# Weight tiles of the second half of the value product, split into buffers of their own

## What is computed

```python
x = x + 0.5 * swiglu(rms_norm(x, p['ffn1_norm']), p['ffn1_w_in'], p['ffn1_w_out'])
h = rms_norm(x, p['mix_norm'])
q, k, v, f, bx_in, by_in, sb, sc, sx, g = split_columns(h @ p['w_in'])
logf = jax.nn.log_sigmoid((f + p['b_forget']).astype(jnp.float32))
o_a = attn_fn(q, k, v, logf)          # logits get c[t] - c[s], c = cumsum(logf)
```

## Time and profile before

| | |
|---|---|
| median of three runs | 3013.25 us (3011.82 to 3015.27) |
| the profiled execution | 3012.57 us |
| its span in the profile | 3010.9 us |
| mean granted TensorE clock | 0.991 |
| busy: PE, DVE, ACT, POOL | 98%, 49%, 33%, 4% |
| HBM over the span | 82 GB/s |

### The profile page before, as it was taken

The page is one execution under the profiler, slowest core; times in us unless marked ns, Lnnn a source line. Parts: engine busy times, 40 slices in busy tenths (PEclk is TensorE's granted clock), DMA queues, the critical chain, the costliest instruction groups (busy, mean ns, idle before and its releaser), DMA issues.

```text
span 3010.9 us, 54957 instructions
## 1 busy us (share of the span) xinstructions
PE 2959.2 (98%) x21632; PEld 2862.5 (95%) x21632; DVE 1465.2 (49%) x2025; ACT 985.3 (33%) x1287; POOL 119.0 (4%) x104
## 2 busy tenths in 40 slices
PE   7999998999999999999999999989999999999999
PEld 6999998888899999999999999988888999999998
DVE  4434355555744544343444444566665454444434
ACT  4212133444633342121332111334445333321113
POOL 1000011000000010000100000100000000000001
PEclk9999999999999999999999999999999999999999
DMA  3222222333222222222222222223332222222222
GB/s 116 84 85 79 77 82 81 84 82 82 71 82 79 91 84 83 75 80 84 85 84 73 88 86 78 84 69 83 81 82 80 84 84 91 73 86 80 84 84 87
DMA packets 299022, 248.82 MB, mean 83 GB/s; under 512 B 20643, under 2 KB 296307, under 8 KB 298919
## 3 DMA queue, kind: packets, MB, share of 16 engines
q1 hardware_dynamic: 296775, 242.44, 26.0%
q0 software_dynamic: 2144, 4.98, 0.5%
HBM read 240.04 MB, written 7.34 MB: 82 GB/s over the span
## 4 chain that ended last, share of the span: by engine, by line
PE 94%; DVE 2%; ACT 1%; issue 1%; DVEq 0%; DMA 0%; POOLq 0%; ACTq 0%; SPq 0%
PE ps L448 85%; PE ps L671 2%; PE ps L616 2%; PE ps L700 1%; DVE tmp L1019 1%; PE ps L661 1%; PE ps L647 1%; PE ps L594 1%; PE ps L617 1%; PE ps L603 0%; PE ps L552 0%; PE ps L553 0%; PE ps L554 0%; DMA xin<-in_x_sample 0%; ACT whi L759 0%
## 5 line engine op out<-in xcount | busy, mean ns | idle before, releaser
L759 ACT ACTIVATE whi<-wraw 128x1024 fp32r<-128x1024 f32 (+1 forms) x456 | 475.1, 1044 | 1610.1 <-PE ps L448 1560.9
L448 PE MATMUL ps<-hh,whi 128*128 128x288 f32 x4480 | 967.1, 298 | 18.5 <-ACT vtok L857 6.1
L448 PE MATMUL ps<-hh,wlo 128*128 128x288 f32 x4480 | 961.9, 296 | 0.0
L448 PE MATMUL ps<-hl,whi 128*128 128x288 f32 x4480 | 961.5, 296 | 0.0
L1013 DVE TENSOR_TENSOR wlo<-wraw,whi 128x1024 fp32r<-128x1024 f32 (+1 forms) x456 | 548.4, 1205 | 457.4 <-ACT whi L759 456.3
L448 PEld LDWEIGHTS ps<-hh,whi 128*128 128x128 f32 x4480 | 724.9, 190 | 25.1 <-ACT vtok L857 6.3
L448 PEld LDWEIGHTS ps<-hh,wlo 128*128 128x128 f32 x4480 | 724.5, 189 | 0.0
L448 PEld LDWEIGHTS ps<-hl,whi 128*128 128x128 f32 x4480 | 724.3, 189 | 0.0
L1047 DVE TENSOR_TENSOR tmp<-tmp,ps 128x576 f32<-128x576 f32 x176 | 132.7, 754 | 509.3 <-PE ps L448 508.4
L448 PE MATMUL ps<-al,whi 128*128 128x288 f32 x1408 | 302.2, 296 | 0.0
L448 PE MATMUL ps<-ah,whi 128*128 128x288 f32 x1408 | 302.1, 296 | 0.0
(11 more groups left out here) (282 smaller groups left out, 2519.8 us busy)
## 6 DMA issues: line engine op xcount, KB each, us to landing
wraw<-in_ffn_w_in SPq DMA_DIRECT2D x88, 1024.0 KB
wraw<-in_ffn_w_out SPq DMA_DIRECT2D x32, 1024.0 KB
wraw<-in_w_in SPq DMA_DIRECT2D x28, 1024.0 KB
wraw<-in_w_in SPq DMA_DIRECT2D x56, 512.0 KB
wraw<-in_ffn_w_out SPq DMA_DIRECT2D x16, 768.0 KB
wraw<-in_w_branch SPq DMA_DIRECT2D x24, 512.0 KB
wraw<-in_w_out SPq DMA_DIRECT2D x9, 1024.0 KB
kv<-in_cache_k SPq DMA_DIRECT2D x128, 64.0 KB, 1.9
```

The source lines that it names most:

```text
L448: last = pe.matmul(ps[slot][:, half, 0:HF], weights, rhs[:, k, half * HF:(half + 1) * HF], start=(start and c == 0 and n == 0), stop=(stop ...
L759: act.activation(split_tile(whi, j, rowwise), raw_tile(slot, j, rowwise), ACT.Copy).then_inc(hi_ready, 1)
```

## The change

Two buffers `vhi` and `vlo` are added, of the shape of `whi` and `wlo`. They are laid over the last part of `kpt` and over `prob`; a placeholder `over_kv` keeps them off `kv` and off `kpt`'s first 512 columns. `values(1)` reads them in place of `whi` and `wlo`. Value tiles 2 and 3 are split into them right behind ffn1, ahead of the square root on ScalarE (with no wait for PSUM) and ahead of its reciprocal on VectorE. The first pair's tiles 0 and 1 take the places at which value tiles 2 and 3 were split, after `values(0)`. Nothing is added to or taken from the computation, the transfers or the number of splits. SyncE's program is the same; what it waits for (`lo_ready`) comes at other times.

```diff
             with ExitStack() as m2:
+
+                sb("over_kv", [P, SB * NPG * P + SEQ], F32, m2)
+                vhi = sb("vhi", [P, 2, KD * P], F32R, m2)
+                vlo = sb("vlo", [P, 2, KD * P], F32R, m2)
+            with ExitStack() as m2:
                 oh = sb("oh", [P, 12, N], F32R, m2)
...
-                            rh = whi[:, :, k * P:(k + 1) * P]
-                            rl = wlo[:, :, k * P:(k + 1) * P]
+                            rh = (whi, vhi)[u][:, :, k * P:(k + 1) * P]
+                            rl = (wlo, vlo)[u][:, :, k * P:(k + 1) * P]
...
-            def split_ahead(st, w, k, L, i=0):
-
-                wait_tile(st, k, L, i)
+            def split_ahead(st, w, k, L, i=0, into=whi):
+
+                if k is not None:
+                    wait_tile(st, k, L, i)
...
                 ffn("ffn1", 0, L)
+                fv = S["fv"]
+                split_ahead(fv, 0, None, L, into=vhi)
+                split_ahead(fv, 1, None, L, into=vhi)
                 root(S["mixnorm"], L)
-                fv = S["fv"]
...
-                split_ahead(fv, 0, 2, L)
-                split_ahead(fv, 1, 2, L)
+                split_ahead(fv, 2, 2, L)
+                split_ahead(fv, 3, 2, L)
...
                     wait_tile(fv, k, L)
-                    if u:
-                        split_ahead(fv, 2, 5, L)
-                        split_ahead(fv, 3, 5, L)
...
-            def split_ahead(st, w, L, i=0):
+            def split_ahead(st, w, L, i=0, hi=whi, lo=wlo):
...
                 ffn("ffn1", 0, L)
+                fv = S["fv"]
+                split_ahead(fv, 0, L, hi=vhi, lo=vlo)
+                split_ahead(fv, 1, L, hi=vhi, lo=vlo)
                 rstd(S["mixnorm"], L).then_inc(rstd_ready, 1)
...
-                    split_ahead(fv, 0, L)
-                    split_ahead(fv, 1, L)
+                    split_ahead(fv, 2, L)
+                    split_ahead(fv, 3, L)
...
-                split_ahead(fv, 2, L)
-                split_ahead(fv, 3, L)
```

More of the change, by code:

```diff
@@ L758, in split_ahead @@
                 act.wait_ge(unit_loaded[slot], L * (plan["layer_units"] // 2 * 32) + i * (st.units // 2 * 32) + (base // 2 + 1) * 32)
-                act.activation(split_tile(whi, j, rowwise), raw_tile(slot, j, rowwise), ACT.Copy).then_inc(hi_ready, 1)
+                act.activation(split_tile(into, j, rowwise), raw_tile(slot, j, rowwise), ACT.Copy).then_inc(hi_ready, 1)
             def root(st, L):
@@ L1012, in split_ahead @@
                 dve.wait_ge(hi_ready, st.unit(0, L, i) * 2 + (w + 3))
-                dve.tensor_tensor(split_tile(wlo, j, rowwise), raw_tile(slot, j, rowwise), split_tile(whi, j, rowwise).bitcast(F32),
+                dve.tensor_tensor(split_tile(lo, j, rowwise), raw_tile(slot, j, rowwise), split_tile(hi, j, rowwise).bitcast(F32),
                                   ALU.subtract).then_inc(lo_ready, 1)
```

## The result

| | before | changed |
|---|---|---|
| median | 3012.98 us (3011.82 to 3015.27, 4 runs) | 2988.76 us (2984.33 to 2991.94, 4 runs) |
| the profiled execution | 3012.57 us | 2984.33 us |
| its span | 3010.9 us | 2982.7 us |
| mean granted clock | 0.991 | 0.995 |

The ratio of the two is 0.9918, with a 95% interval of 0.9903 to 0.9933: 24.2 us less in the medians. The forecast was 2988.3 us, and "faster". The profiled execution of the changed kernel is the fastest of its four, 4.4 us under their median, so between the two profiles there are 28.2 us of span, not 24.2.

A forecast was written before the change was run, and what follows sets the result against it. TensorE's own work plus its idle stretches and the half speed behind them were taken as the bound; five terms sum to 24.9 us, so 3013.25 - 24.9 = 2988.3 us, range 2983.5 to 2996.

The forecast's parts named there:

- What bounds the kernel: TensorE, 98% busy: a change that adds no matmul can act only through the places where it stands still.
- Terms 1 and 2: Ahead of `values(1)`, both layers: 11.57 us of waiting for VectorE's low parts goes, and 3.39 us of half speed behind it.
- term 5: TensorE's followers start before the last matmul ends: some 0.15 us at each of four places, 0.6 us, an estimate.
- Terms 3 and 4: At the first pair's first tile, both layers: 6.10 us of waiting for `vtok` copies goes, and 3.21 us of half speed.
- the third step: The 6.10 us wait goes: the pair's splits leave the place ahead of ScalarE's copies for the value tiles' old slots.
- The covers: Moved splits cost nothing: 1.4 us of cover ahead of ScalarE's root, 2.0 us ahead of VectorE's reciprocal.
- The loads: SyncE's loads of the pair's second and third units go out near 466 and 488 instead of 488 and 508, costing nothing.
- The clock falls without a wait: Rival, 10%: the clock still falls at the joins of transposes and small products, some 1.6 us each; 2990 to 2995 us.
- Luck in the attention: Rival, 6%: shifted timing gives one to three fewer clock falls in the attention, 1.6 us each; 2983.5 to 2986.7 us.
- the other rivals: Second wait stays, 2997.7 us, 3%; or low parts count only with the pair's, so `values(1)` waits, 3003.6 us, 2%.
- the slower rival: Chance 2%: moved splits delay root, forget logs and `lf`; from about 22 us of delay slower, 26 us late gives 3021.

The follow-up runs named there:

- swap_only: The kernel before, without new buffers, with ScalarE's copies into `vtok` ahead of the splits of the pair's tiles: 3009.28 us, ratio 0.9986.
- late_root: The changed kernel with eight more copies of a raw tile into `vhi` on ScalarE ahead of the two real ones: 2998.11 us, ratio 0.9951 against the kernel before.
- thin_half: The changed kernel with transposes ahead of `weighted(0)` and the thin matmuls halved around it: 2977.53 us, ratio 0.9887 against the kernel before.
- after_again: The changed kernel run once more with no edit: 2986.45 us, ratio 0.992 against the kernel before.
- thin_moved: The changed kernel with transposes ahead of `weighted(0)` and all thin matmuls behind it: 2987.86 us, ratio 0.9922 against the kernel before.
- thin_half_again: The changed kernel with thin matmuls halved around `weighted(0)`, measured a second time: 2975.49 us, ratio 0.988 against the kernel before.
- before_thin: The kernel before with only the attention order of halved thin matmuls around `weighted(0)`, nothing of the change: 3001.08 us, ratio 0.9967.
- no_buffers: The kernel before with `vtok` copies ahead of the pair's splits and VectorE's value splits ahead of the polynomial in `log1p`: 3002.33 us, ratio 0.9969.

## Why the prediction was right, point by point

**What bounds the kernel** held: the change adds no matmul and removes none, and the time follows TensorE's idle stretches and clock.

**Terms 1 and 2** (first wait and the half speed behind it, 7.7 us in layer 1 and 7.2 in layer 2, with 0.15 of term 5 each): measured from start to start 8.24 and 22.77 - 15.01 = 7.76 us. They are 0.4 us larger than said: `values(1)` takes 495.08 - 480.87 = 14.21 us, where I had taken the 14.48 of `values(0)`, whose first two matmuls start 0.34 us apart and not 0.12. The small error is that I took the length of one product for the other's.

**Terms 3 and 4** (second wait and its half speed, 4.65 us a layer, 4.80 with term 5): 4.63 and 11.97 - 7.33 = 4.64 us. The pair's first tile takes 502.41 - 495.91 = 6.50 us (said 6.4). **Term 5**, an estimate, was small and about right: `values(1)` starts 0.46 us behind the first of the five transposes.

**That the two waits need each other** was in the third step only in half a sentence (the pair's splits go to the slots where the value tiles' were). swap_only shows how much hangs on it: 2.4 us alone.

**The covers.** ScalarE, changed kernel, first layer, answers to the earlier trace rows:

```profile
461.13 1.99 ACT L765 ACTIVATE vhi<-wraw 128x1024 fp32r<-128x1024 f32 x2
463.14 1.28 ACT L769 ACT_TABLE_LOAD   x1
466.01 0.74 ACT L769 ACTIVATE tmp<-ps,eps 128x576 f32<-128x576 f32 x1 [1.59 <-PE ps L467]
...
480.47 2.01 ACT L765 ACTIVATE whi<-wraw 128x1024 fp32r<-128x1024 f32 x2 [5.63 <-PE ps L559]
...
492.55 1.57 ACT L862 ACTIVATE vtok<-ps,small 128x256 f32<-128x256 f32 x4 [7.67 <-PE ps L559]
```

The splits follow at once, with no bracket, so the raw unit had landed; the root still waits 1.59 us for TensorE (said 1.4). The four copies end at 494.12, and TensorE asks at 495.91: 1.8 us to spare, where 1.9 were said, still the tightest place.

VectorE, first layer, answers to the earlier trace rows (the first two low parts together, and the first of them alone):

```profile
460.91 0.82 DVE L1039 SCALAR_TENSOR_TENSOR hl<-x,gains,hh  x1
462.20 3.03 DVE L1018 TENSOR_TENSOR vlo<-wraw,vhi 128x1024 fp32r<-128x1024 f32 x2 [0.48 <-ACT vhi L765]
462.20 1.90 DVE L1018 TENSOR_TENSOR vlo<-wraw,vhi 128x1024 fp32r<-128x1024 f32 x1 [0.48 <-ACT vhi L765]
466.78 3.75 DVE L1024 RECIPROCAL tmp<-tmp 128x576 f32<-128x576 f32 x1 [1.55 <-ACT tmp L769]
...
490.75 0.75 DVE L1175 SCALAR_TENSOR_TENSOR lf<-tmp 16x576 f32<-16x576 f32 x1
```

Here a size was off: I had the two low parts at the 2.34 us of the earlier trace rows, and they took 3.03, so the reciprocal had 1.55 us of cover and not 2.0. The extra is in the first of them, 1.90 us. GpSimd is the reason that fits. Its timeline:

```profile
461.30 1.72 POOL L1424 TENSOR_TENSOR tmp<-tmp 128x576 f32<-128x576 f32 x1 [3.06 <-ACT tmp L785]
```

It adds squares for the norm until 463.02, 0.8 us into the low part, and the low part lost 0.7 us. The second layer has the same overlap and the same 3.0 us. In late_root, where the same pair comes nine microseconds later and GpSimd is done, both took 2.36 us. The Trainium skill, "SBUF — State Buffer", section "SBUF: two separate sides", has a rule for it: a VectorE instruction with two SBUF inputs and a GpSimd instruction that reads SBUF exclude each other for the whole instruction. By that rule, the loss is the overlap, 0.8 us, and the trace agrees (0.7). It cost nothing, as the reciprocal waited anyway.

`lf` is ready at 491.50 and TensorE comes at 495.29, 3.8 us later (said 4.0); late_root shows that this is the true margin.

**The loads.** SyncE, first layer, answers to the earlier trace rows; in the changed kernel:

```profile
465.45 1.00 SPq L345 DMA_DIRECT2D wraw<-in_w_in  x2
...
487.07 1.00 SPq L345 DMA_DIRECT2D wraw<-in_w_in  x2
```

They go out near 466 and 487, as said, and no wait of TensorE for a load came of it.

**The rivals.** *The clock falls without a wait* at the joins: it didn't. The window over both joins has 1.00, and thin_half has ten transposes followed by 1.9 us of thin matmuls at 1.00. The rule of the Trainium skill cited there, "TensorE: Matmul & The Clock Gate", section "Part 4: PE-mode transpose", may hold, but stretches of about 1 us that hold only transposes and small products don't bring the clock down here. *Luck in the attention*: there was none between the two profiles, which both spend 23.9 us at half speed there, though in other pairs; the luck of the profiled execution, two falls or 3.4 us, lies at the first blocks of the layers. Of the other rivals no mechanism showed. late_root takes the slower rival's path with nine microseconds of delay and stays 13.9 us faster than the kernel before. The rival's break-even of some 22 us wasn't tried; it left out the half speed behind such a wait, by which 7.6 us of waiting cost 11.7, so it lies lower.

**What stays open**: why runs of the same kernel differ in the number of falls (before 3005.7 to 3015.8 on one chip, the changed kernel 2984.5 to 2988.2). Two profiles of the changed kernel, this one and after_again's, have the same 23.9 us at half speed but not at the same places (one of the falls of after_again is near the start). What decides whether a thin stretch or a short wait brings a fall isn't shown.

## What to carry to other kernels

Price an idle stretch of TensorE with what follows it: here 5.8 us of waiting cost about 8 and 3.05 us cost 4.6, because the clock had fallen and came back late. When a wait names a low part or a copy, look at what stands ahead of it in that engine's own order (four steps of a polynomial, two splits for the next stage) before giving it a buffer; a buffer pays when the producer's place moves with it, and when what takes the vacated place removes a second wait. And look for falls where the engine is busy: read the granted clock beside the busy share, and mix thin matmuls with wide ones.

## What the runs showed of the hardware

- TensorE's clock falls to 1.2 GHz while the engine is wholly busy, at or behind 32 matmuls of 16 columns in one stretch (3.6 to 4.5 us), in six of eight pairs of the changed kernel and of thin_moved, with ten transposes or with a full product ahead. In two stretches of 1.9 us with eight products of 128 to 512 columns between them it doesn't, in none of the eight pairs of thin_half, thin_half_again and before_thin. A fall lasts 3.4 us at the half level, or 6.8.
- Every idle stretch of TensorE of 3.05 us or more in this stage, 16 in the profiles of the six kernels that have any, went with half speed. For shorter ones the length doesn't decide. In no_buffers 2.87 us were followed by 0.50 in the first layer and by 1.00 in the second; 2.27 us were followed by 1.00 in the first and by 0.50 in the second, and in swap_only likewise (windows 508 to 509: 1.00, 1989 to 1990: 0.50). Near the start 1.94 us (before) were followed by a fall and 2.96 us (changed kernel) were not. So shortening a wait can gain more than the wait, but not surely.
- A 128x1024 subtraction on VectorE took 1.90 us instead of about 1.2 while GpSimd added 128x576 squares for its first 0.8 us.
